# A depthwise convolution's running sums move from SBUF to PSUM, its gate product moves to VectorE, and two jobs on GpSimd change places

## The reference

```
h = modulate(rms_norm(x, g_mix), sh1, sc1);  z = h @ w_in          # 1024 -> 1536: u | v | gt, 512 each
d = trailing means of u over 2/4/8/16 rows - u;   pool_out = (d @ w_pool per group) * pool_scale
a = v * sigmoid(gt)                                                 # the gate-value product
yc = causal depthwise conv of a, 31 taps, per channel, + b_dw
conv_out = silu(layer_norm(yc))
x = x + g1 * (concat(pool_out, conv_out) @ w_out)
h2 = modulate(rms_norm(x, g_ffn), sh2, sc2)
idx, wts = route(h2)              # sigmoid scores of 64 experts, best 8 of the 4 best groups
x = x + g2 * (routed_experts(h2, idx, wts) + shared expert);  y = modulate(rms_norm(x))
```

## Time and profile before

| what | value |
|---|---|
| median of three runs | 3183.2 us |
| the profiled execution, its own time | 3187.95 us |
| its span, first to last instruction | 3186.2 us |
| granted TensorE clock, mean | 0.927 |
| busy: PE, DVE, ACT, POOL | 2689.8, 1750.1, 1059.0, 1116.8 us |
| convolution taps 1 to 30 (L916), 960 instructions | 380.7 us |
| gate-value products (L510), 32 instructions | 224.2 us |

### The profile page before, as it was taken

The page is one execution under the profiler, slowest core; times in us unless marked ns, Lnnn a source line. Parts: engine busy times, 40 slices in busy tenths (PEclk is TensorE's granted clock), DMA queues, the critical chain, the costliest instruction groups (busy, mean ns, idle before and its releaser), DMA issues.

```text
span 3186.2 us, 56600 instructions
## 1 busy us (share of the span) xinstructions
PE 2689.8 (84%) x11753; PEld 2016.8 (63%) x11754; DVE 1750.1 (55%) x3603; ACT 1059.0 (33%) x2213; POOL 1116.8 (35%) x1173
## 2 busy tenths in 40 slices
PE   6896797777777847998999999899999999999980
PEld 1184664554565626877777777777777777777760
DVE  1034785775786754255554466565655455445538
ACT  1022212112111113244443455454544344334422
POOL 0035525645743242323323232223323232233326
PEclk9998898898887768999999999999999999999995
DMA  7851001001010306568777678888886776667767
GB/s 269 299 230 46 27 34 53 20 34 60 0 40 34 113 13 193 109 179 253 210 209 200 183 217 256 242 235 253 246 263 184 208 215 182 184 184 217 191 175 249
DMA packets 255795, 518.50 MB, mean 163 GB/s; under 512 B 18222, under 2 KB 154375, under 8 KB 255588
## 3 DMA queue, kind: packets, MB, share of 16 engines
q1 hardware_dynamic: 199108, 327.34, 29.8%
q0 software_dynamic: 56624, 190.48, 25.2%
HBM read 386.48 MB, written 131.99 MB: 163 GB/s over the span
## 4 chain that ended last, share of the span: by engine, by line
PE 52%; POOL 13%; DMA 13%; issue 9%; DVE 6%; ACT 4%; ACTq 2%; POOLq 1%; DVEq 1%; SPq 0%
PE zb L1484 21%; PE mx L1484 11%; PE zb L1318 7%; POOL b_av L510 7%; DMA b_xg<-hf_d,b_gidx 6%; PE tp L1497 4%; POOL list_d L520 4%; DMA acc_d<-b_ob,b_sidx 4%; PE mx L1340 3%; PE zb L1282 2%; ACT b_wh L810 2%; DMA b_big<-in_w_ada 1%; PE zb L1433 1%; DVE b_wl L1181 1%; POOL b_pa L493 1%
## 5 line engine op out<-in xcount | busy, mean ns | idle before, releaser
L604 POOL DMA_INDIRECT acc_d<-b_ob,b_sidx x180 | 311.2, 1729 | 1086.9 <-DVE b_ob L1206 565.6
L1484 PE MATMUL zb<-b_wh,b_xh 128*128 x1448 | 590.6, 408 | 52.4 <-issue 33.7
L1484 PE MATMUL zb<-b_wh,b_xl 128*128 x1448 | 573.1, 396 | 0.0
L1484 PE MATMUL zb<-b_wl,b_xh 128*128 x1448 | 572.7, 396 | 0.0
L1181 DVE TENSOR_TENSOR b_wl<-b_win,b_wh (+1 forms) x780 | 481.3, 687 | 133.5 <-ACT b_wh L810 133.4
L810 ACT CAST b_wh<-b_win (+1 forms) x780 | 419.7, 621 | 150.2 <-issue 113.6
L1318 PE MATMUL zb<-b_hT,b_win 128*128 128x256 f32 x1536 | 364.4, 402 | 95.4 <-ACT b_sgt L687 94.6
L1318 PEld LDWEIGHTS zb<-b_hT,b_win 128*128 128x128 f32 x1536 | 310.0, 203 | 149.0 <-ACT b_sgt L687 97.4
L916 DVE SCALAR_TENSOR_TENSOR b_y<-b_a_buf,b_wdw,b_y 128x256 f32<-128x256 f32 x960 | 380.7, 484 | 0.0
L1484 PEld LDWEIGHTS zb<-b_wh,b_xh 128*128 128x128 f32 x1448 | 273.8, 189 | 130.4 <-issue 71.6
L1158 DVE SCALAR_TENSOR_TENSOR b_hh<-b_sgx,b_lt,zb 128x256 f32<-128x256 f32 x181 | 87.0, 481 | 473.8 <-ACT b_sgx L795 472.9
(11 more groups left out here) (245 smaller groups left out, 3154.7 us busy)
## 6 DMA issues: line engine op xcount, KB each, us to landing
b_win<-in_w_gate SPq DMA_DIRECT2D x64, 1024.0 KB, 6.5
b_win<-in_w_up SPq DMA_DIRECT2D x64, 1024.0 KB, 12.4
b_win<-in_w_down SPq DMA_DIRECT2D x64, 1024.0 KB, 14.5
b_big<-in_w_ada SPq DMA_DIRECT2D x12, 2048.0 KB, 8.8
...
```

The source lines that it names most:

```text
L604: G.indirect_dma_start(acc_d, bass.IndirectOffsetOnAxis(ap=sidx[1 - j][:, 0:1], axis=0), ob[1 - j][:], None, compute_op=ALU.add).then_inc( ...
L1484: last = M.matmul(o, lhs, rhs, start=(first and n == 0), stop=(final and n == len(terms) - 1))
```

## The change

It does four things.

1. The product `sgt * vv` is taken off POOL. DVE does it for all four chunks in one instruction that writes straight into `a_buf`, in place of the copy from `av`. `sgt` and `vv` get four buffers, so ACT waits once per step (until DVE has taken the last step's product) and not per chunk.
2. The convolution's running sum lies in the PSUM bank `ms`, which holds two chunks. So chunks 0 and 1 go through all 31 taps, then chunks 2 and 3; the last tap writes `y` in SBUF. Each instruction waits for the one two places ahead of it; before it was the one four places ahead.
3. Router logits and ranks move from `ms` to `ly`, where y's transposes lie too; PE gets waits that keep these users apart.
4. On POOL, the four `diff` stand together, the scatter follows them, and the powers for the layer norm come behind the scatter.

```diff
-        def amul(s, j, post):
-            zv = z.now + (CH if post else 0) + CH + 2 * j + 1
-            pool.wait_ge(S["z_drained"], zv + 1)
-            if post:
-                pool.wait_ge(S["a_taken"], s)
-            G.tensor_tensor(av[:, j, :], sgt[:, j % 2, :], vv[:, j % 2, :], ALU.mult).then_inc(S["a_ready"], 1)
...
             if has_in:
-                for j in range(CH):
-                    amul(s, j, has_post)
-                    if j < CH - 1:
-                        diff(s, j, first, has_post)
+                for g_ in range(CH):
+                    diff(s, g_, first, has_post)
+            z.step((CH if has_post else 0) + (ZC if has_in else 0) + (TPS if has_post else 0))
+            if has_scatter:
+                scatter(s - 3)
             if has_post:
                 for j in range(TPS):
                     power(st[:, 6:7], st[:, 7:8], S["lnv"], lt_i.now + j + 1, S["lnr"])
-            if has_in:
-                diff(s, CH - 1, first, has_post)
-            z.step((CH if has_post else 0) + (ZC if has_in else 0) + (TPS if has_post else 0))
-            if has_scatter:
-                scatter(s - 3)
...
-                if not (first and j < 2):
-                    act.wait_ge(S["a_ready"], CH * s + j - 1)
-                A.activation(sgt[:, j % 2, :], zb[z.n % 2][:, 0:SUP], ACT.Sigmoid).then_inc(S["z_drained"], 1)
+                if j == 0 and not first:
+                    act.wait_ge(S["a_taken"], s)
+                A.activation(sgt[:, j, :], zb[z.n % 2][:, 0:SUP], ACT.Sigmoid).then_inc(S["z_drained"], 1)
...
-            A.activation(sg_r[0:nt, j, :], ms[0:nt, 0:NE], ACT.Sigmoid).then_inc(S["lg_drained"], 1)
+            A.activation(sg_r[0:nt, j, :], ly[0:nt, 0:NE], ACT.Sigmoid).then_inc(S["lg_drained"], 1)
...
-            dve.wait_ge(S["a_ready"], CH * p + CH)
+            dve.wait_ge(S["z_drained"], ZC if first else (CH + ZC + TPS) * p + ZC - TPS)
             if not first:
                 chain(V.tensor_copy(a_buf[:, :, 0:CONVB], a_buf[:, :, SUP:SUP + CONVB]))
-            V.tensor_copy(a_buf[:, :, CONVB:CONVB + SUP], av[:]).then_inc(S["a_taken"], 1)
+            V.tensor_tensor(a_buf[:, :, CONVB:CONVB + SUP], sgt[:], vv[:], ALU.mult).then_inc(S["a_taken"], 1)
             dve.wait_ge(S["a_taken"], p + 1)
-            if not first:
-                dve.wait_ge(S["ly_filled"], ti.now)
-            for k in range(TAPS):
-                for c in range(CH):
...
+            for c2 in range(0, CH, 2):
+                for k in range(TAPS):
+                    if c2 == 0 and k == TAPS - 1 and not first:
+                        dve.wait_ge(S["ly_filled"], ti.now)
+                    for c in (c2, c2 + 1):
+                        win_, acc = a_buf[:, c, k:k + SUP], ms[:, (c - c2) * SUP:(c - c2 + 1) * SUP]
+                        if not (first and c2 == k == 0):
+                            dve.wait_ge(S["conv_link"], cv.now - 1)
+                        if k == 0:
+                            ins = V.tensor_scalar(acc, win_, wdw[:, c, 0:1], vecT[:, c:c + 1], ALU.mult, ALU.add)
+                        else:
+                            ins = V.scalar_tensor_tensor(acc if k < TAPS - 1 else y[:, c, :], win_, wdw[:, c, k:k + 1], acc, ALU.mult, ALU.add)
+                        ins.then_inc(S["conv_link"], 1)
+                        cv.step()
...
-        def y_T(i, src, c0, nt=P):
+        def y_T(i, src, c0, scored, nt=P):
             wait(pe, S["ly_drained"], i)
+            wait(pe, S["lg_drained"], scored)
+            wait(pe, S["rk_drained"], kd.now)
...
-        def logits(i, nt=P):
+        def logits(i, normed, nt=P):
             pe.wait_ge(S["tp_drained"], 2 * tpu.now)
             wait(pe, S["lg_drained"], i)
             wait(pe, S["rk_drained"], kd.now)
+            wait(pe, S["ly_drained"], normed)
             for k in range(KD):
-                last = M.matmul(ms[0:nt, 0:NE], h2T[:, k, 0:nt], w_router[:, k, :], start=(k == 0), stop=(k == KD - 1))
+                last = M.matmul(ly[0:nt, 0:NE], h2T[:, k, 0:nt], w_router[:, k, :], start=(k == 0), stop=(k == KD - 1))
```

More of the change, by code:

```diff
@@ L148, in program @@
         mix_filled mix_drained lg_filled lg_drained rk_filled rk_drained xsq xms xrs xn_ready lnv lnr
-        x1_ready x1_sq x1_ms x1_rs h2_ready a_ready a_taken d_ready conv_link m_ready pairs_ready
+        x1_ready x1_sq x1_ms x1_rs h2_ready a_taken d_ready conv_link m_ready pairs_ready
         pool_const dve_const sm_x sm_h sm_state sm_y edge_tp edge_ready
@@ L174, in program @@
     hT = f("hT", [P, KD, SUP])
-    av = f("av", [P, CH, SUP]); a_buf = f("a_buf", [P, CH, CONVB + SUP]); u_buf = f("u_buf", [P, CH, POOLB + SUP])
+    a_buf = f("a_buf", [P, CH, CONVB + SUP]); u_buf = f("u_buf", [P, CH, POOLB + SUP])
     y = f("y", [P, CH, SUP]); dd = f("dd", [P, CH, SUP]); mixP = f("mixP", [P, CH, SUP]); mixC = f("mixC", [P, TPS, CH, P])
-    sgt = f("sgt", [P, 2, SUP]); vv = f("vv", [P, 2, SUP]); pa = f("pa", [P, 2, POOLB + SUP])
+    sgt = f("sgt", [P, CH, SUP]); vv = f("vv", [P, CH, SUP]); pa = f("pa", [P, 2, POOLB + SUP])
     xin = [f("xin0", [P, D]), f("xin1", [P, D])]; xres = f("xres", [P, D]); x1b = f("x1b", [P, D]); h2 = f("h2", [P, D])
@@ L684, in win_drain @@
                 act.wait_ge(S["zw_filled"], wn.step())
-                if not (first and j < 2):
-                    act.wait_ge(S["a_ready"], CH * s + j - 1)
-                A.activation(sgt[:, j % 2, :], zb[z.n % 2][:, 0:SUP], ACT.Sigmoid).then_inc(S["z_drained"], 1)
+                if j == 0 and not first:
+                    act.wait_ge(S["a_taken"], s)
+                A.activation(sgt[:, j, :], zb[z.n % 2][:, 0:SUP], ACT.Sigmoid).then_inc(S["z_drained"], 1)
                 z.step()
                 act.wait_ge(S["zw_filled"], wn.step())
-                A.copy(vv[:, j % 2, :], zb[z.n % 2][:, 0:SUP]).then_inc(S["z_drained"], 1)
+                A.copy(vv[:, j, :], zb[z.n % 2][:, 0:SUP]).then_inc(S["z_drained"], 1)
                 z.step()
@@ L900, in conv @@
         def conv(p, first):
-            dve.wait_ge(S["a_ready"], CH * p + CH)
+            dve.wait_ge(S["z_drained"], ZC if first else (CH + ZC + TPS) * p + ZC - TPS)
             if not first:
                 chain(V.tensor_copy(a_buf[:, :, 0:CONVB], a_buf[:, :, SUP:SUP + CONVB]))
-            V.tensor_copy(a_buf[:, :, CONVB:CONVB + SUP], av[:]).then_inc(S["a_taken"], 1)
+            V.tensor_tensor(a_buf[:, :, CONVB:CONVB + SUP], sgt[:], vv[:], ALU.mult).then_inc(S["a_taken"], 1)
             dve.wait_ge(S["a_taken"], p + 1)
-            if not first:
-                dve.wait_ge(S["ly_filled"], ti.now)
-            for k in range(TAPS):
-                for c in range(CH):
-                    win_ = a_buf[:, c, k:k + SUP]
-                    if k == 0:
-                        ins = V.tensor_scalar(y[:, c, :], win_, wdw[:, c, 0:1], vecT[:, c:c + 1], ALU.mult, ALU.add)
-                    else:
-                        dve.wait_ge(S["conv_link"], cv.now - CH + 1)
-                        ins = V.scalar_tensor_tensor(y[:, c, :], win_, wdw[:, c, k:k + 1], y[:, c, :], ALU.mult, ALU.add)
-                    ins.then_inc(S["conv_link"], 1)
-                    cv.step()
+            for c2 in range(0, CH, 2):
[12 more added lines that the diff above has]
+                        cv.step()
         def norm(i, nt=P):
@@ L1000, in slots @@
             dve.wait_ge(S["rk_filled"], group + 1)
-            V.tensor_copy(ri[n, 0, w], ms[:, NE:3 * NE].rearrange("p (t e) -> p t e", t=TPS)[n, w]).then_inc(S["rk_drained"], 1)
+            V.tensor_copy(ri[n, 0, w], ly[:, NE:3 * NE].rearrange("p (t e) -> p t e", t=TPS)[n, w]).then_inc(S["rk_drained"], 1)
             for t in range(tiles):
@@ L1361, in ranks @@
             for t in range(tiles):
-                o = ms[0:nt, (1 + t) * NE:(2 + t) * NE]
+                o = ly[0:nt, (1 + t) * NE:(2 + t) * NE]
                 M.matmul(o, ones[:, 0:nt], Macc[:], start=True, stop=False)
@@ L1379, in step @@
                 h_T(i - 1)
-                logits(i - 1)
+                logits(i - 1, i)
             if has_in:
@@ L1386, in step @@
                 pe.wait_ge(S["conv_link"], CH * TAPS * s)
-                y_T(i, y, 0)
+                y_T(i, y, 0, i if has_late else 0)
             if has_next:
@@ L1392, in step @@
                 z0 = z.now
-                y_T(i + 1, y, P)
+                y_T(i + 1, y, P, i if has_late else 0)
                 w_out_mm(i, 0, z0)
@@ L1399, in step @@
                 h_T(i)
-                logits(i)
+                logits(i, i + TPS)
                 ti.step(TPS)
@@ L1442, in _ @@
         h_T(NTILE - 1)
-        logits(NTILE - 1)
+        logits(NTILE - 1, NTILE)
         pe.wait_ge(S["sm_y"], 1)
         pool_mm(NSUP, dsm, NS)
-        y_T(NTILE, ysm, 0, NS)
+        y_T(NTILE, ysm, 0, NTILE, NS)
         yn_T(NTILE, NS)
@@ L1463, in _ @@
         h_T(NTILE, NS)
-        logits(NTILE, NS)
+        logits(NTILE, NTILE + 1, NS)
```

## The result

The changed kernel took 3098.44 us (median of four runs, 3089.53 to 3101.72), the kernel before on the same chip 3184.95 (four runs, 3181.33 to 3189.03): a ratio of 0.9715, 95% interval 0.9701 to 0.9730. The same changed kernel, run once more as e0_after_again, took 3090.1 us (five runs), a ratio of 0.9695 (0.9682 to 0.9708).

What follows compares the result with a forecast made beforehand. It took the front to be bound by a ring of waits, with POOL held by DVE's two-SBUF-input taps. 79.4 - 8.6 + 7 + 16.7 = 94.5 us off the 3183.2 median gave 3089 us, range 3060 to 3155.

Steps and rivals of the forecast that it cites:

- The wait before the transpose: DVE's idle time before the first norm: PE's w_in ends earlier, so y's transpose follows the convolution at once; 79.4 us off.
- POOL is held all the same: Rival, chance 0.03: POOL still waits for DVE's taps, so diffs and scatter delay the norm's power; 3290 us.
- DVE's extra: Product in place of copy, +0.54, and tap 0 into PSUM, +0.53 us a step; 8.6 us more over 8 steps.
- the pace of the taps: DVE's convolution: stays 0.397 us an instruction with the sum in PSUM; bounds -6.8 to +13.7 us a step.
- A dearer PSUM tap: Rival, chance 0.12: each convolution tap is 65 ns slower in PSUM, 62 us given back; 3151 us.
- one bank can't be read and written at once: Rival, chance 0.07, in each tap's inner loop: a tap costs 0.267 us more, +248 us; 3336 us.
- ACT's term: ACT's drains, table load and silu between y's transpose and w_out: 8.33 us falls to 7.4 in step 5; 7 us off.
- The scatter: POOL's 16 DMAs move under the convolution and no longer delay the second norm's power in steps 3 to 7; 16.7 us off.
- The shared bank: New PE waits on `ly`, shared by y's transposes, ranks and logits: cost nothing; 1 to 2 us a step if one bit.
- PE becomes the bound: Rival, chance 0.06: PE's w_in groups run at the slower rate after idling and end past the convolution; 3110 us.
- The idle before the statistics: DVE's idle time before the stats instruction, a sign to check: falls from 97.7 to about 18 us.

Runs made afterwards that it cites:

- e0_after_again: The changed kernel run once more with nothing different: 3090.10 us, ratio 0.9695 to before.
- e9: Kernel before with only the convolution's running sum moved to PSUM by pairs; product on POOL and POOL's order as before: 3111.47 us, ratio 0.9767.
- e1: Changed kernel with the running sum of the taps back in SBUF, the rest of the change kept: 3209.56 us, ratio 1.0062 to before.
- e3: Changed kernel with only the scatter back behind the layer norm's powers, all four diffs still ahead: 3095.62 us, ratio 0.9711 to before.
- e4: Changed kernel with one chunk at a time through all taps, each tap waiting for the one right ahead: 3225.43 us, ratio 1.0112 to before.
- e5: Changed kernel with 4 overwritten matmuls added in steps 1 to 7 before PE's wait for the convolution: 3091.03 us, ratio 0.9699 to before.
- e8: Changed kernel with the product back on POOL, in the order diffs, first product, scatter, other three products, powers: 3089.51 us, ratio 0.9690 to before.
- e7: Kernel before with only POOL's order changed, fourth diff and scatter ahead of the layer norm's powers: 3318.72 us, ratio 1.0405.
- e2: Changed kernel with the product back on POOL, product and diff of each chunk in turn, then scatter, then powers: 3181.36 us, ratio 0.9982 to before.

## Why the prediction was right

The forecast was 3089 us with a range of 3060 to 3155; 3098 and 3090 came. Over the eight steps, term by term (sums over steps 1 to 8 between the places named in the prediction, read from the two timelines):

| term | forecast us | trace us |
|---|---|---|
| wait from convolution's end to y's transpose | -79.4 | 81.53 to 1.29: -80.2 |
| product and taps longer | +8.6 | 397.28 to 401.49: +4.2 |
| ACT between transpose and w_out | -7 | 64.13 to 59.62: -4.5 |
| w_out's first tile to its second | 0 | 141.61 to 145.23: +3.6 |
| scatter, second w_out to L943 | -16.7 | 168.11 to 151.42: -16.7 |
| sum | -94.5 | -93.4, with +0.26 from there to the next step |

That the sum is right to 1 us is luck: DVE's extra was 4.4 us smaller than forecast, and the two terms around w_out 6.1 us worse. The first and the last term, which make up the gain, are right by themselves.

- *The wait before the transpose* and the reason for it hold. e9 shows that the sum's place alone gives 79.4 us of front, e1 that without it 117.7 are lost. The rival "POOL is held all the same" is out: beside the PSUM taps POOL's tensor instructions keep their 0.20 to 0.87 us, and the DMA issues (0.95 to 2.05 us) are as in e3, where they run away from the taps.
- *DVE's extra* was mis-sized, +0.53 us a step instead of +1.07. The two parts that I priced held: the product +0.54, and tap 0 +0.52, since from its first start to the first start of the next taps two now take 0.91 us and four took 1.30, 0.455 a piece against 0.325. The term that I put at nothing is the pace of the taps: 0.392 us against 0.396 from start to start, -0.53 a step. "A dearer PSUM tap" and "one bank can't be read and written at once" are both out. From the Trainium skill's "Perfetto Trace Analysis", section "Optimizing Scalar/DVE Operations", it would follow that the accumulator in PSUM costs 65 ns more a tap, an estimate from its two figures; in these series it costs 4 ns less. Whether the page's difference shows where each tap waits for its own neighbour, no run tells: in e4 a tap takes (66.6 - 1.4)/124 = 0.526 us (the prediction's upper bound was 0.51), and no run has the same with the sum in SBUF.
- *ACT's term* was 2.5 us short. PE now idles 3.34 to 6.93 us before y's transpose in steps 1 to 7, and what it does next runs at the lower of its two levels. The windows of the transposes and of w_out's first block (columns as above), and last that of the first block in step 5 of the kernel before:

```profile
673.60:681.40 7.80, 4.80 (x21) 4.00 (x21) 2.88 (x7) 5.69 (x13) 0.95 (x2) 0.50 0.36 134
681.40:686.60 5.20, 5.20 (x9) 2.31 (x10) 3.88 (x31) 0.00 (x0) 0.17 (x1) 0.69 0.00 0
...
740.40:745.30 4.90, 4.90 (x8) 2.18 (x9) 3.80 (x31) 0.00 (x0) 3.93 (x6) 0.71 0.00 0
```

  A granted clock of 0.50 is the level of 1.2 GHz. y's transpose takes 1.11 us where I took 0.60, so the norm waits 1.21, not 0.7, and ACT's stretch is 7.78 us, not 7.4. e5 shows that this is the cause: in its steps 2 to 6, where the transpose takes 0.66 us, the stretch is 6.91.
- *w_out's first tile to its second* I put at no change; it takes 3.6 us more. The first block of eight takes 5.14 to 6.60 us over the steps, against 3.60 for the blocks behind it, at a granted clock of 1.00. But it was slow before as well, 5.12 to 5.52 us, at nearly the same clock in step 5 (0.71 and 0.69). PE's idle time before the transpose isn't the whole reason for the rest: in step 8 it is only 0.52 us and the transpose takes 0.63, and still the block takes 6.39 us where it took 5.52; in e5 the block got longer while the transposes got quicker. Why the low clock reaches further into this block is open.
- *The scatter* came out to the tenth, but its reason was half right. I priced it as the scatter's move. The runs say that the loss needed the fourth diff and the scatter together behind the layer norm's powers (e9 to e8, 18.0 us of front); with the diffs ahead, the scatter's own place is worth nothing (e3), and the diff without a scatter cost nothing either. The cover I gave for it, 4 to 12 us, was 13.
- *The shared bank* I priced at nothing. It costs 0.5 us once: in step 8 the transpose waits for the logits' sigmoid, as PE's timeline shows:

```profile
976.77 0.63 PE L1316 MATMUL ly<-b_ident,b_y 128*128 128x128 f32 x4 [0.52 <-ACT b_sg_r L704]
```

- "PE becomes the bound" didn't happen in that form: PE idles 3.34 to 6.93 us before y's transpose in steps 1 to 7.
- *The idle before the statistics* was forecast at about 18 us and is 24.9 for the 16 prompt tiles: the first norms keep 9.0 (1.21 us in most steps, not 0.7), the second ones 15.9, where I had counted 12.2 as staying; both wait for transposes at the lower clock.
- The profiled executions differ by 3187.95 - 3097.76 = 90.2 us: the 93.4 of the table, less 3.15 by which step 1 starts later in the changed kernel's profile, in a stretch that the change doesn't touch (0.95 in e0_after_again). The rest of the way to the median is the spread of the runs.

What the change amounts to, taken in the order e9, e8, changed kernel: the sum's place 79 us, POOL's order 18, the product on DVE -4. In another order the shares differ, as e7 and e2 show.
